# Attention value products with V stationary, two query tiles side by side, sums divided out later

## The chip, the cores and the metric

The kernel runs on one core of a Trainium2 chip. The metric is the device time of one execution in microseconds (us); three runs of the kernel before gave a median of 2039.84 us (2039.72 to 2040.91). The core has a matrix engine (TensorE, PE in the rows; PEld is its weight load), a vector engine (DVE), a scalar engine (ACT), a general engine (POOL), and a sync engine (SP) that here only issues DMAs. Each runs its own list of instructions in order and waits on semaphores that others raise. SBUF is the working memory of 128 partitions, PSUM the memory of 128 partitions into which PE writes.

## The reference, cut to what matters

The program is two transformer-like blocks on one sequence of 1024 tokens with 1024 channels, all in float32. The change is in the attention of the first block and in one product of the second. The attention has 8 heads of 64 channels; three dilated causal windows are combined by the softmax of their log-sums:

```python
sc = jnp.einsum('xhnqd,xhnkd->xhnqk', qb, kb).astype(jnp.float32) * scale
sc = jnp.where(valid, sc + bias[:, None], NEG_INF)
m = jnp.max(sc, axis=-1, keepdims=True)
p = jnp.exp(sc - m)
den = jnp.sum(p, axis=-1, keepdims=True)
o = jnp.einsum('xhnqk,xhnkd->xhnqd', p, vb.astype(jnp.float32)) / den
...
wts = jax.nn.softmax(jnp.stack(lses, axis=0), axis=0)
o_att = jnp.sum(wts[..., None] * jnp.stack(outs, axis=0), axis=0)
y_att = o_att @ w_proj_att
...
merged = jax.nn.sigmoid(g_att + gb_att) * y_att + jax.nn.sigmoid(g_ssm + gb_ssm) * y_ssm
```

Three windows with one softmax over them are one softmax over all causal keys with a bias that counts in how many windows a key lies, and this is how the kernel computes it. In the second block, a causal 128x128 matrix per group mixes the tokens of each chunk:

```python
sg = jnp.einsum('gts,bnsgc->bntgc', w_m, vc) + b_s.T[:, :, None]
```

## The kernel before, in words

Large products run with each float32 operand split into a high and a low part (type fp32r) and take three matmuls per pair of tiles; PE does them in a fixed written order, and POOL and ACT make the split weights ahead of it. The attention stands at 226 to 544 us of the span.

It walks over 64 tiles, `tiles`: a head and a block of 128 queries, `qb` from 0 to 7. A tile needs the `qb + 1` key blocks of 128 up to its own. Before, the tiles of a head go long, short, long, short (7, 0, 6, 1, 5, 2, 4, 3). Tile t goes through these steps, software-pipelined over the engines:

- `scores(t)` on PE (line 1380) writes q times k into PSUM slot t % 2.
- `smallest(t)` on DVE (line 2598) adds the bias and takes the minimum of the negated scores.
- `softmax(t)` on ACT (line 1938) takes the exponential and its sum `den`.
- `transposes(t)` on PE (lines 1394 and 1400) turns each 128x128 block of the weights into slot 2.
- `near_half(t)` on DVE (line 2608, first four blocks of a long tile) and `transposed(t)` on ACT (line 1952, the rest) copy them to SBUF.
- `values(t)` on PE (line 1419) multiplies by V: the turned weights are the stationary 128x128 operand, 64 columns of V move, and 128 queries by 64 channels come out.
- `normalised(t)` on DVE (lines 2614 and 2621) takes the reciprocal of `den` and multiplies into `o_tok`.

In PE's list one iteration t is `scores(t+3)`, `gate_part(t+1)`, `transposes(t+1)`, `values(t)`. A gate part (line 1194) is 12 large matmuls of another product, the gates, interleaved here; two parts fill one PSUM bank, `gate_logits` on ACT (line 1964) reads it, and the next part waits for that (`gate_read`). Every fourth iteration has four small matmuls `ada` (line 1292), whose operand DVE adds up in `ada_chunks` (line 2636). At the end `out_transposes` (line 1437) turns `o_tok` to channels by tokens, and `o_high` on ACT and `o_low` on DVE split it for the projection (`product`, line 1108).

SP's queue (the loop at line 670) issues loads at fixed places of the same loop over t, each behind a wait. Behind the loop it loads `ys_h` and `ys_l` (lines 699 and 700), the output of the state-space branch, whose four landings PE awaits (`y_in`) before the projection; then the gates come back (line 709).

The spatial product of the second block (`spatial`, line 1576) is 16 matmuls in each of four units, V-like operand stationary with 64 columns, group 0 for all eight token tiles and then group 1.

Of the kernel before, what the change touches and what calls it, by code (L numbers as in the profile page):

```python
# [169 lines left out]
def build(nc, a, out):  # L170
    ctx = ExitStack()
    with ctx:
# [110 lines left out]
        prob_long = at("prob_long", [P, 2, T], 160 * kib)  # L283
        prob_short = at("prob_short", [P, 2, HALF], 168 * kib)
        pt_long = at("pt_long", [P, T], 172 * kib)
        pt_short = at("pt_short", [P, HALF], 176 * kib)
        gate_st = at("gate_st", [P, 2, HALF], 178 * kib)
        ada_part = at("ada_part", [P, 2, NB], 182 * kib)
        o_tok = at("o_tok", [P, QB, ATT], 184 * kib)
        neg_max = at("neg_max", [P, 4], 204 * kib)  # L290
        den = at("den", [P, 4], 204 * kib + 32)
        rden = at("rden", [P, 4], 204 * kib + 64)
# [8 lines left out]
        gate_in = at("gate_in", [P, 2, 2, T], 184 * kib)  # L301
# [27 lines left out]
        tiles = [(h, qb) for h in range(HEADS) for long in range(QB - 1, QB // 2 - 1, -1) for qb in (long, QB - 1 - long)]  # L329
# [4 lines left out]
        def prob_of(t):  # L334
            return (prob_short if t % 2 else prob_long)[:, t // 2 % 2, :]

        def prob_t_of(t):
            return pt_short if t % 2 else pt_long
# [12 lines left out]
        v_d = nc.dram_tensor("v_scratch", [QB, P, ATT], F32).ap()  # L351
        ysh_d = nc.dram_tensor("ysh_scratch", [2, P, T], F32).ap()
# [8 lines left out]
            p_ready pt0 pt1 ptc0 ptc1 pv o_ready otr oh_ready ot_ready proj_read mix_ready mh_ready  # L361
# [35 lines left out]

        op_ready = (op_in, later(64)), beyond(f_in[0], 64 + 32 + 32), (op_in, later(64 + 32))
# [98 lines left out]
        def _(sp):  # L497
# [172 lines left out]
            for t in range(NT):  # L670
# [7 lines left out]
                if t in (NT // 4 + 1, NT // 2 + 1):  # L678
                    pair = t // (2 * NH) + 1
                    sp.wait_ge(s["pv"], AHEAD + 2 * NH * (pair - 1))  # L680
# [21 lines left out]
            def gates(j):  # L702
                for th in range(2):
                    sp.wait_ge(gate_out[th], AHEAD + 16 * (KD + 2 * j + 2))
                for cg in range(2):
                    if j:
                        sp.wait_ge(s["proj_read"], AHEAD + 2 * j + cg - 1)
                    for g in range(2):
                        sp.dma_start(gate_in[:, cg, g, :], gates_d[g * KD + 2 * j + cg]).then_inc(gate_back[cg], 16)

            sp.wait_ge(s["otr"], KA)
# [385 lines left out]
        def _(pe):  # L1097
# [84 lines left out]
            def gate_part(i):  # L1182
# [9 lines left out]
                for c in range(KD // 2 * part, KD // 2 * part + KD // 2):  # L1192
                    for p, (w, x) in enumerate(((w_h, act_h), (w_h, act_l), (w_l, act_h))):
                        last = nc.tensor.matmul(slot(1)[:, HALF:T], w[:, n % 2, c, P * (j % 2):P * (j % 2) + P], x[:, c, tok],  # L1194
# [189 lines left out]
            def transposes(t):  # L1384
# [4 lines left out]
                if t % 2:  # L1389
                    pe.wait_ge(s["ptc0"], t // 2 + 1)  # L1390
                elif t:
                    pe.wait_ge(s["ptshort"], t // 2)
# [3 lines left out]
                if qb >= 4:  # L1396
                    if t:
                        pe.wait_ge(s["ptc1"], t // 2)
# [4 lines left out]
            def values(t):  # L1403

                h, qb = tiles[t]
                pair = h // 2
                if qb >= 4:
                    pe.wait_ge(s["ptc0"], t // 2 + 1)
                    pe.wait_ge(s["ptc1"], t // 2 + 1)
                else:  # L1410
                    pe.wait_ge(s["ptshort"], t // 2 + 1)
                if t % (2 * NH) == 0:
                    pe.wait_ge(v_in[pair % 2], 16 * (pair // 2 + 1))
                if t >= 2:
                    pe.wait_ge(s["o_ready"], AHEAD + t - 1)
                dst = slot(3)[:, HALF * (t % 2):HALF * (t % 2) + HALF]
                src = prob_t_of(t)
# [5 lines left out]
                if t % 4 == 3:  # L1423
                    k = t // 4
                    pe.wait_ge(s["ada_summed"], SUMMED + k + 1)
                    ada(dst[:, HD:HD + 2], ada_part[:, k % 2]).then_inc(s["ada_done"], 1)

            for t in range(2):
                scores(t)
            gate_part(0)  # L1430
# [3 lines left out]
            def out_transposes(c, dst):  # L1434

                for t in range(QB):
                    last = nc.tensor.transpose(dst[:, P * t:P * t + P], o_tok[:, t, P * c:P * c + P], ident[:])
                last.then_inc(s["otr"], 1)
# [1779 lines left out]
```

## Time and profile before

| | us |
|---|---|
| median of three runs | 2039.84 |
| profiled execution, its own time | 2037.9 |
| its span, first to last instruction | 2036.2 |
| PE busy in the span | 2004.8 |
| attention, 226 to 544 of the span | 318 |

Busy times of one engine merge instructions that overlap. Matmuls are pipelined, so the mean duration of one is longer than the distance from one start to the next; what a group costs is read from the start of its first to the start of what follows. A float32 matmul leaves two records, each a weight load and a matmul, so 288 products leave 576.

### The profile page before, as it was taken

What the parts mean: (1) busy time and instruction counts of PE and PEld (TensorE: products, weight loads), DVE (VectorE), ACT (ScalarE), POOL (GpSimd) and SP (SyncE); (2) the same over time, 40 slices, a digit from 0 to 9 for tenths busy, and PEclk for the clock granted to TensorE, in tenths of its full rate; (3) what the DMA queues carried; (4) which work ended last, traced back from release to release, by engine and by line L of the source; (5) the groups of instructions that cost most, each with busy time, mean ns of one, the idle gap of its engine ahead of it and who ended that gap; (6) DMA issues with size and microseconds to landing.
All of it is one profiled execution on the core that took longest, in us unless ns stands there. A gap on an engine that the chain in (4) does not pass through costs nothing. (4 is left out here: it accounts for less than half of the span.)

```text
span 2036.2 us, 25850 instructions
## 1 busy us (share of the span) xinstructions
PE 2004.8 (98%) x10079; PEld 1678.1 (82%) x10079; DVE 1070.7 (53%) x1381; ACT 646.8 (32%) x1068; POOL 1303.7 (64%) x757
## 2 busy tenths in 40 slices
PE   7999999999999999999999999999999999999998
PEld 4788988888888887788888888888888888887888
DVE  5971355556472495655622377721563555525554
ACT  4212332232331364444300045433434533311103
POOL 2648445756165539999945456876887888849650
PEclk9999999999999999999999999999999999999999
DMA  9545645444445213233474241343234222098332
GB/s 370 147 104 155 207 136 165 148 142 136 176 145 186 92 43 119 100 112 120 178 289 170 94 145 30 116 141 108 72 115 145 103 104 104 32 355 309 131 135 83
DMA packets 188360, 293.24 MB, mean 144 GB/s; under 512 B 12920, under 2 KB 136784, under 8 KB 188240
## 3 DMA queue, kind: packets, MB, share of 16 engines
q1 hardware_dynamic: 178256, 268.53, 38.9%
q10 hardware_dynamic: 9984, 23.07, 2.9%
q8 instruction: 80, 1.31, 0.3%
q14 instruction: 40, 0.33, 0.1%
HBM read 211.64 MB, written 79.94 MB: 143 GB/s over the span
## 5 line engine op out<-in xcount | busy, mean ns | idle before, releaser
L964 POOL TENSOR_SCALAR w_h<-raw 128x512 fp32r<-128x512 f32 (+2 forms) x108 | 237.0, 2194 | 332.3 <-issue 155.3
L1505 PE MATMUL ps<-tb,w_h 128*128 128x512 f32 x1344 | 416.9, 391 | 4.2 <-DVE quads L2772 3.6
L1050 POOL TENSOR_TENSOR w_l<-raw,w_h 128x512 fp32r<-128x512 f32 x210 | 310.1, 1486 | 99.3 <-ACT w_h L2062 99.3
L1505 PEld LDWEIGHTS ps<-tb,w_h 128*128 128x128 f32 x1344 | 251.3, 188 | 60.8 <-DVE quads L2772 5.2
L1505 PE MATMUL ps<-tb,w_l 128*128 128x512 f32 x672 | 261.6, 389 | 0.0
L966 POOL TENSOR_TENSOR w_l<-raw,w_h 128x512 fp32r<-128x512 f32 (+2 forms) x108 | 200.6, 1857 | 9.0
L2062 ACT ACTIVATE w_h<-raw 128x512 fp32r<-128x512 f32 x210 | 130.8, 628 | 236.1 <-PE ps L1505 153.5
L1505 PE MATMUL ps<-act_h,w_h 128*128 128x512 f32 x504 | 196.3, 389 | 0.6 <-ACT quads L2091 0.5
L1505 PE MATMUL ps<-act_l,w_h 128*128 128x512 f32 x504 | 196.1, 389 | 0.0
L1505 PE MATMUL ps<-act_h,w_l 128*128 128x512 f32 x504 | 196.1, 389 | 0.0
L1505 PEld LDWEIGHTS ps<-tb,w_l 128*128 128x128 f32 x672 | 126.1, 188 | 26.2
L1108 PE MATMUL ps<-act_h,w_h 128*128 128x512 f32 x352 | 139.1, 395 | 2.4 <-POOL w_l L966 1.6
L1108 PE MATMUL ps<-act_h,w_l 128*128 128x512 f32 x352 | 137.1, 389 | 0.0
L1108 PE MATMUL ps<-act_l,w_h 128*128 128x512 f32 x352 | 137.0, 389 | 0.0
L1505 PEld LDWEIGHTS ps<-act_h,w_h 128*128 128x128 f32 x504 | 94.6, 188 | 21.1 <-ACT quads L2091 0.9
L1505 PEld LDWEIGHTS ps<-act_l,w_h 128*128 128x128 f32 x504 | 94.6, 188 | 19.7
L1505 PEld LDWEIGHTS ps<-act_h,w_l 128*128 128x128 f32 x504 | 94.6, 188 | 19.5
L1194 PE MATMUL ps<-act_h,w_h 128*128 128x512 f32 x256 | 100.3, 392 | 0.0
L1194 PE MATMUL ps<-act_l,w_h 128*128 128x512 f32 x256 | 100.1, 391 | 0.0
L1194 PE MATMUL ps<-act_h,w_l 128*128 128x512 f32 x256 | 100.1, 391 | 0.0
L995 POOL TENSOR_SCALAR k_hh<-q 128x1024 fp32r<-128x1024 f32 x8 | 22.2, 2773 | 115.7 <-DMA k_ll<-qk_scratch 115.7
L1050 POOL TENSOR_TENSOR w_l<-sum,w_h 128x512 fp32r<-128x512 f32 x56 | 79.3, 1417 | 20.6 <-ACT w_h L2062 18.8
(412 smaller groups left out, 4554.3 us busy)
## 6 DMA issues: line engine op xcount, KB each, us to landing
raw<-in_w_in SPq DMA_DIRECT2D x44, 1024.0 KB, 5.2
raw<-in_w_up SPq DMA_DIRECT2D x16, 1024.0 KB, 5.2
f_scratch<-r SPq DMA_DIRECT2D x16, 1024.0 KB, 8.2
gates_scratch<-quads SPq DMA_DIRECT2D x24, 512.0 KB, 7.6
r<-gates_scratch SPq DMA_DIRECT2D x12, 1024.0 KB, 7.0
ada_lo<-in_w_ada SPq DMA_DIRECT2D x16, 512.0 KB, 3.6
ada_hi<-in_w_ada SPq DMA_DIRECT2D x16, 512.0 KB, 3.9
gates_scratch<-gate_st ACTq DMA_DIRECT2D x32, 256.0 KB, 2.2
```

The costliest lines, as they stand in the source:

```text
L964: nc.gpsimd.tensor_scalar(w_h[:, k, c, :], src[:, c, :], 1.0, None, ALU.mult).then_inc(s["w_high"], 1)
L966: nc.gpsimd.tensor_tensor(w_l[:, k, c, :], src[:, c, :], w_h[:, k, c, :].bitcast(F32), ALU.subtract).then_inc(done, 1)
L995: stage_step(nc.gpsimd.tensor_scalar(k_hh[:, e, :], q.bitcast(F32), 1.0, None, ALU.mult))
L1050: nc.gpsimd.tensor_tensor(w7_l[:, SLOTS[o]], x, w7_h[:, SLOTS[o]].bitcast(F32), ALU.subtract)\
L1108: last = nc.tensor.matmul(dst[:, tok], w[:, k, kw + c, P * cg:P * cg + P], x[:, c, tok], start=(c == 0 and p == 0), stop=(c == kc - 1 and ...
L1194: last = nc.tensor.matmul(slot(1)[:, HALF:T], w[:, n % 2, c, P * (j % 2):P * (j % 2) + P], x[:, c, tok], start=(c == 0 and p == 0), stop=( ...
L1505: last = nc.tensor.matmul(bank_of(n, bank), w[:, SLOTS[o], c, :], x(c), start=(first and c == 0 and p == 0), stop=(c == KD // 2 - 1 and p ...
L2062: A.activation(w7_h[:, SLOTS[o]], src, ACT.Copy).then_inc(s["w7_high"], 1)
```

## The change

Seven edits:

- The tiles of a head go from long to short, 7 down to 0, and the weights use three buffers by turns.
- `values(u)` takes two neighbouring tiles, 2u and 2u+1. The 64 columns of V are stationary and 128 query columns move; tile 2u's result goes to PSUM partitions 0 to 63, tile 2u+1's to 64 to 127, block by block in turn. The result is channels by queries, so `out_transposes` is gone.
- DVE copies the result undivided to `o_raw` (`read_values`), and the division comes later: every fourth tile DVE takes reciprocals of 4 x 128 sums, SP stores them to memory (`rden_scratch`) and reads them back spread over 64 partitions (`over_den`), and DVE multiplies half a head at a time.
- The gate bank moves from slot 1 to slot 3, and ACT reads it ahead of its copy of the turned weights.
- In the last iterations the gate parts, `o_high`, `o_low` stand elsewhere, and the projection does both `ys` products before the first attention product.
- The gates read back go to two other places in SBUF, with other waits before them.
- `spatial` alternates the two groups within a token tile.

```diff
-        tiles = [(h, qb) for h in range(HEADS) for long in range(QB - 1, QB // 2 - 1, -1) for qb in (long, QB - 1 - long)]
+        tiles = [(h, qb) for h in range(HEADS) for qb in range(QB - 1, -1, -1)]
...
+                if t % 4 == 2:
+                    sp.wait_ge(*beyond(rden_ready, t // 4 + 1))
+                    sp.dma_start(rden_d[t // 4].rearrange("(b p) -> p b", p=P), rden[:, t // 4 % 2, :], allow_slow_non_contiguous=True)                      .then_inc(rden_out[0], 16)
+                if t % 4 == 3:
+                    i = t // 4
+                    sp.wait_ge(*beyond(rden_out, 16 * (i + 1)))
+                    if i:
+                        sp.wait_ge(*beyond(o_norm, i))
+                    sp.dma_start(over_den[head_rows(i // 2), :], rden_d[i].partition_broadcast(HD)).then_inc(rden_in[0], 16)
...
-            sp.wait_ge(s["otr"], KA)
+            sp.wait_ge(s["sm_ready"], AHEAD + NT)
+            sp.wait_ge(s["ot_ready"], 2)
             gates(0)
...
-                for b in range(qb + 1):
-                    last = nc.tensor.matmul(dst[:, 0:HD], src[:, P * b:P * b + P],
-                                            v_st[:, pair % 2, b, HD * (h % 2):HD * (h % 2) + HD],
-                                            start=(b == 0), stop=(b == qb))
+                if u:
+                    pe.wait_ge(s["o_ready"], AHEAD + 2 * u)
+                if u % 2:
+                    pe.wait_ge(s["ada_summed"], SUMMED + u // 2 + 1)
+                    ada(slot(3)[:, P:P + 2], ada_parts[u // 2 % 2]).then_inc(s["ada_done"], 1)
+                elif u:
+                    pe.wait_ge(s["mod2_ready"], u // 2)
+                for b in range(tiles[2 * u][1] + 1):
+                    for i in range(2):
+                        if b <= tiles[2 * u + i][1]:
+                            last = nc.tensor.matmul(slot(3)[HD * i:HD * i + HD, 0:P],
+                                                    v_st[:, pair % 2, b, head_rows(h)], prob_t_of(2 * u + i)[:, P * b:P * b + P],
+                                                    start=(b == 0), stop=(b == tiles[2 * u + i][1]))
...
             for t in range(NT):
                 if t + 3 < NT:
                     scores(t + 3)
                 if t + 1 < NT - 2:
                     gate_part(t + 1)
+                if t >= NT - 2:
+                    gate_part(t)
+                if t % 2:
+                    values(t // 2)
                 if t + 1 < NT:
                     transposes(t + 1)
-                if t == NT - 3:
-                    pe.wait_ge(s["sm_ready"], AHEAD + NT - 1)
-                    pe.wait_ge(s["o_ready"], AHEAD + 2 * NH)
-                    out_transposes(0, slot(0))
-                if t == NT - 2:
-                    gate_part(NT - 2)
-                values(t)
-            pe.wait_ge(s["ptshort"], NT // 2)
-            out_transposes(1, slot(2))
-            gate_part(NT - 1)
-            pe.wait_ge(s["o_ready"], AHEAD + NT)
-            out_transposes(2, slot(3))
-            pe.wait_ge(s["ot_ready"], 2)
-            out_transposes(3, slot(2))
...
-                    product(slot(2 * cg + 1), (N_PROJ + j) % 2, cg, 2, ys_h, ys_l, kw=KA).then_inc(s["gemm"], 1)
-                    first = s["ot_ready"] if j == 0 and cg == 0 else None
-                    product(slot(2 * cg), (N_PROJ + j) % 2, cg, KA, o_h, o_l, each=first).then_inc(s["gemm"], 1)
+                        pe.wait_ge(s["mod2_ready"], NT // 4)
+                    product(slot(2 * cg + 1), (N_PROJ + j) % 2, cg, 2, ys_h, ys_l, kw=KA)
+                    if j:
+                        product(slot(2 * cg), (N_PROJ + j) % 2, cg, KA, o_h, o_l).then_inc(s["gemm"], 2)
+                if j == 0:
+                    for cg in range(2):
+                        product(slot(2 * cg), N_PROJ % 2, cg, KA, o_h, o_l, each=None if cg else s["ot_ready"]).then_inc(s["gemm"], 2)
...
-                for g in range(2):
-                    grp = 2 * c + g
-                    for t in range(QB):
+                for t in range(QB):
+                    for g in range(2):
+                        grp = 2 * c + g
...
+                if t % 2 == 0 and t < NT - 2:
+                    gate_logits(t // 2)
                 if t + 1 < NT:
                     transposed(t + 1)
-                if t % 2 == 0 and t < NT - 2:
-                    gate_logits(t // 2)
                 if t + 2 < NT:
                     softmax(t + 2)
...
-                if t % 2 and t + 1 < NT:
-                    near_half(t + 1)
                 if t + 3 < NT:
                     smallest(t + 3)
                 ada_chunks(t // 4, ((0, 1, 2), (3, 4, 5), (6, 7), ())[t % 4])
-                normalised(t)
-                if t == NT - 3:
-                    o_low(0, slot(0))
-            o_low(1, slot(2))
-            o_low(2, slot(3))
-            o_low(3, slot(2))
+                if t % 4 == 2:
+                    over_denominators(t // 4)
+                if t % 2:
+                    read_values(t // 2)
+                if t + 1 < NT and is_long(t + 1):
+                    near_half(t + 1)
+                if t % 4 == 1 and t >= 4:
+                    normalised(t // 4 - 1)
+                if t >= NT - 2:
+                    o_low(t - (NT - 2))
+            normalised(NT // 4 - 1)
+            for c in range(2, KA):
+                o_low(c)
```

How instructions stand on three engines, before and now. First PE in the middle of a head, without the 12 gate matmuls between the groups. Before, transposes of a short tile (`prob_short`), the value products of a long one (five blocks), and scores of a later one:

```order
L1394 MATMUL ps<-ident,prob_short 128x128 x4
L1419 MATMUL ps<-v_st,pt_long 128x64 x5
L1380 MATMUL ps<-k_hh,q_124 128x512
L1380 MATMUL ps<-k_ll,q_124 128x512
L1380 MATMUL ps<-k_hh,q_124 128x384
```

Now, in an odd iteration, the last gate matmul of a part, the value products of two tiles (four and three blocks), the transposes of the next tile, and scores:

```order
L1220 MATMUL ps<-act_h,w_l 128x512
L1449 MATMUL ps<-prob_t,v_st 64x128 x7
L1418 MATMUL ps<-ident,prob 128x128 x2
L1406 MATMUL ps<-k_hh,q_124 128x512
L1406 MATMUL ps<-k_ll,q_124 128x512
```

The value products moved ahead of the transposes, stand only in every second iteration, and have output shape 64x128 in place of 128x64. Next ACT in the same region, where `gate_st` is the read of the gate bank, `pt_long` and `pt_short` (now `prob_t`) the copies of the turned weights. Before:

```order
L1952 ACTIVATE pt_short<-ps 128x256 [waits pv,pt0]
L1964 ACTIVATE gate_st<-ps,cols_a 128x512 [waits gemm,gate_out1]
L1938 ACTIVATE prob_long,den<-prob_long,neg_max 128x768 [waits o_ready,sm_ready]
L1952 ACTIVATE pt_long<-ps 128x256 [waits pv,pt1]
L1938 ACTIVATE prob_short,den<-prob_short,neg_max 128x384 [waits o_ready,sm_ready]
L1971 DMA gates_scratch<-gate_st 128x512 [waits gate_read]
```

Now:

```order
L1980 ACTIVATE gate_st<-ps,cols_a 128x512 [waits gemm,gate_out1]
L1968 ACTIVATE prob_t<-ps 128x128 [waits pv,pt1]
L1954 ACTIVATE prob,den<-prob,neg_max 128x512 [waits sm_ready]
L1968 ACTIVATE prob_t<-ps 128x512 [waits pv,pt0]
L1954 ACTIVATE prob,den<-prob,neg_max 128x384 [waits sm_ready]
L1987 DMA gates_scratch<-gate_st 128x512 [waits gate_read]
```

The gate read moved from behind the copy to ahead of it. Last, SP's queue at the end of the attention, where `ada_hi` is a load of the small products, `ys_h` and `ys_l` the state-space output. Before:

```order
L632 DMA ada_hi<-in_w_ada 128x4x256 [waits ada_summed]
L640 DMA raw<-in_w_proj_att 128x4x256 [waits w_split]
L642 DMA raw<-in_w_proj_ssm 128x2x256
L699 DMA ys_h<-ysh_scratch 128x1024 [waits y_spill,s_ready]
L700 DMA ys_l<-ysl_scratch 128x1024
```

Now (`colt_read` is the semaphore of `rden_ready`, `const_in` that of `rden_out`, `c_ready` that of `o_norm`):

```order
L656 DMA raw<-in_w_proj_att 128x4x256 [waits w_split]
L658 DMA raw<-in_w_proj_ssm 128x2x256
L714 DMA over_den<-rden_scratch 64x512 [waits c_ready,const_in]
L708 DMA rden_scratch<-rden 128x4x1 [waits colt_read]
L714 DMA over_den<-rden_scratch 64x512 [waits c_ready,const_in]
L724 DMA ys_h<-ysh_scratch 128x1024 [waits y_spill,s_ready]
L725 DMA ys_l<-ysl_scratch 128x1024
```

The last two stores and spreads of the sums now stand between the last weight load and the `ys` loads.

## Rows read from the trace of the kernel before

**Rows 1.** Page, engines: busy time, share of the span, instructions

```profile
PE 2004.8 (98%) x10079; PEld 1678.1 (82%) x10079; DVE 1070.7 (53%) x1381; ACT 646.8 (32%) x1068; POOL 1303.7 (64%) x757
```

**Rows 2.** Windows: us, busy us of each engine (instructions), clock, DMA share, GB/s

```profile
300.00:340.00 40.00, 40.00 (x243) 35.08 (x242) 24.99 (x56) 12.37 (x30) 23.54 (x9) 1.00 0.52 162
1340.00:1362.30 22.30, 22.30 (x116) 18.58 (x114) 4.59 (x6) 7.55 (x13) 14.46 (x12) 1.00 0.38 118
```

**Rows 3.** Groups by line: records, busy us, mean ns of one, idle before

```profile
L1419 PE MATMUL ps<-v_st,pt_long 128*128 128x64 f32 x416 | 50.0, 271 | 0.0
...
L1419 PE MATMUL ps<-v_st,pt_short 128*128 128x64 f32 x160 | 21.4, 265 | 0.0
...
L1236 PE MATMUL ps<-u_c,drive 128*64 128x128 f32 x64 | 3.7, 274 | 0.0
```

**Rows 4.** Timeline, PE: value products; columns start us, us, engine, line, operation, tiles

```profile
387.55 1.00 PE L1419 MATMUL ps<-v_st,pt_short 128*128 128x64 f32 x8
388.39 0.56 PE L1292 MATMUL ps<-ones,ada_part 128*128 128x1 f32 x4
...
391.99 1.90 PE L1419 MATMUL ps<-v_st,pt_long 128*128 128x64 f32 x16
393.70 0.48 PE L1380 MATMUL ps<-k_hh,q 128*128 128x512 f32 x1
```

**Rows 5.** Timeline, PE: state-space input, 64 columns stationary, column halves alternating

```profile
105.80 0.39 PE L1108 MATMUL ps<-act_h,w_l 128*128 128x512 f32 x1
106.12 3.71 PE L1236 MATMUL ps<-u_c,drive 128*64 128x128 f32 x64
109.77 0.50 PE L1108 MATMUL ps<-act_h,w_h 128*128 128x512 f32 x1
110.10 0.40 PE L1108 MATMUL ps<-act_l,w_h 128*128 128x512 f32 x1
```

**Rows 6.** Timeline, PE: one unit of the spatial products

```profile
1339.81 3.33 PE L1576 MATMUL ps<-wst,vg 128*64 128x128 f32 x32
1343.07 0.73 PE L1505 MATMUL ps<-tb,w_h 128*128 128x512 f32 x2
```

**Rows 7.** Timeline, PE: the last gate matmul, the transposes behind it, the projection

```profile
542.64 0.39 PE L1194 MATMUL ps<-act_h,w_l 128*128 128x512 f32 x1
542.87 1.91 PE L1437 MATMUL ps<-ident,o_tok 128*128 128x128 f32 x16
544.54 0.47 PE L1108 MATMUL ps<-ys_h,w_h 128*128 128x512 f32 x1
```

**Rows 8.** Timeline, ACT and PE: PE waiting for ACT, and ACT for PE

```profile
531.27 0.20 ACT L1938 ACTIVATION_READ_ACCUMULATOR prob_long<-prob_long,neg_max 128x1 f32 x1
...
531.52 0.66 PE L1394 MATMUL ps<-ident,prob_long 128*128 128x128 f32 x4 [0.68 <-ACT prob_long L1938]
...
543.13 0.69 ACT L1964 ACTIVATE gate_st<-ps,cols_a 128x512 f32<-128x512 f32 x1 [1.81 <-PE ps L1194]
```

**Rows 9.** Timeline, DVE at the end of attention

```profile
535.90 1.00 DVE L2636 SCALAR_TENSOR_TENSOR ada_part<-ada_hi,c_act,ada_part 128x256 f32<-128x256 f32 x2
...
538.28 0.28 DVE L2621 TENSOR_SCALAR o_tok<-ps,rden 128x64 f32<-128x64 f32 x1
...
541.36 1.23 DVE L2655 TENSOR_TENSOR o_l<-ps,o_h 128x1024 fp32r<-128x1024 f32 x1 [1.57 <-ACT o_h L1976]
```

**Rows 10.** Timeline, SP's queue: first and last of the four ys loads

```profile
526.50 0.34 SPq L699 DMA_DIRECT2D ys_h<-ysh_scratch  x1
...
527.83 0.43 SPq L700 DMA_DIRECT2D ys_l<-ysl_scratch  x1
```

**Rows 11.** The ys_l loads (line 700), time to landing

```profile
DMA to landing us min/median/max: 4.5/5.6/6.6
```

**Rows 12.** DMA issues: KB each, median us from issue to landing

```profile
taps_scratch<-taps_s SPq DMA_DIRECT2D x8, 16.0 KB, 1.8
```

**Rows 13.** PE's longest wait: us in total, times, longest us

```profile
PE ps L1274 <- DMA x_tok<-in_x: 3.8, 1, 3.8
```

More of the change, by code:

```diff
@@ L334, in prob_of, with is_long, longs, shorts @@
         def prob_of(t):
-            return (prob_short if t % 2 else prob_long)[:, t // 2 % 2, :]
+            return prob[:, (t + 2) % 3, :]
         def prob_t_of(t):
-            return pt_short if t % 2 else pt_long
+            return prob_t[:, t % 2, :]
+        def is_long(t):
+            return tiles[t][1] >= 4
+        def longs(t):
+            return sum(is_long(i) for i in range(t + 1))
+        def shorts(t):
+            return t + 1 - longs(t)
+        def head_rows(h):
+            return slice(HD * (h % 2), HD * (h % 2) + HD)
+        def token_half(i):
+            return slice(0, HALF) if i % 2 else slice(HALF, T)
         ps = ctx.enter_context(nc.psum_tensor("ps", [P, 4, T], F32))
@@ L679, in _ @@
                     pair = t // (2 * NH) + 1
-                    sp.wait_ge(s["pv"], AHEAD + 2 * NH * (pair - 1))
+                    sp.wait_ge(s["pv"], AHEAD + NH * (pair - 1))
                     for k in range(2):
@@ L1401, in transposes, with values @@
                     last.then_inc(s["pt1"], 1)
-            def values(t):
-                h, qb = tiles[t]
+            def values(u):
+                t = 2 * u + 1
+                h = tiles[t][0]
                 pair = h // 2
-                if qb >= 4:
-                    pe.wait_ge(s["ptc0"], t // 2 + 1)
-                    pe.wait_ge(s["ptc1"], t // 2 + 1)
-                else:
-                    pe.wait_ge(s["ptshort"], t // 2 + 1)
-                if t % (2 * NH) == 0:
+                if is_long(t):
+                    pe.wait_ge(s["ptc0"], longs(t))
+                    pe.wait_ge(s["ptc1"], longs(t))
+                else:
+                    pe.wait_ge(s["ptshort"], shorts(t))
+                if t // (2 * NH) != (t - 2) // (2 * NH):
@@ L2606, in near_half @@
                 if t >= 2:
[L2607 to L2622 removed]
+                    dve.wait_ge(s["pv"], AHEAD + t // 2)
@@ new lines, in near_half, with read_values @@
+                v.tensor_copy(prob_t_of(t)[:, 0:HALF], slot(2)[:, 0:HALF]).then_inc(s["ptc0"], 1)
+            def read_values(u):
+                h = tiles[2 * u][0]
+                dve.wait_ge(s["pv"], AHEAD + u + 1)
+                for i in range(2):
+                    qb = tiles[2 * u + i][1]
+                    v.tensor_copy(o_raw[head_rows(h), h // 2, P * qb:P * qb + P],
+                                  slot(3)[HD * i:HD * i + HD, 0:P]).then_inc(s["o_ready"], 1)
+                if u % 2:
+                    lo = 2 * N_ADA_EARLY + 2 * (u // 2)
+                    dve.wait_ge(s["ada_done"], ADA_DONE + u // 2 + 1)
+                    v.tensor_tensor(mod[:, lo:lo + 2], slot(3)[:, P:P + 2], col_a("b_ada", lo, 2), ALU.add)\
+                     .then_inc(s["mod2_ready"], 1)
@@ new lines, in over_denominators, with normalised @@
+            def over_denominators(i):
+                h, lo = i // 2, 0 if i % 2 else QB // 2
+                dve.wait_ge(s["p_ready"], 4 * i + 4)
+                if i >= 2:
+                    dve.wait_ge(*beyond(rden_out, 16 * (i - 1)))
+                v.reciprocal(rden[:, i % 2, :], den[:, h % 2, lo:lo + QB // 2]).then_inc(rden_ready[0], 1)
+            def normalised(i):
+                h = i // 2
+                x = o_raw[head_rows(h), h // 2, token_half(i)]
+                dve.wait_ge(*beyond(rden_in, 16 * (i + 1)))
+                dve.wait_ge(s["o_ready"], AHEAD + 4 * i + 4)
+                v.tensor_tensor(x, x, over_den[head_rows(h), :], ALU.mult).then_inc(o_norm[0], 1)
@@ L2624, in ada_chunks @@
             def ada_chunks(k, chunks):
-                part = ada_part[:, k % 2]
+                part = ada_parts[k % 2][:]
                 for c in chunks:
```

114 lines of the change are left out of this document (44 added, 70 removed).

## The prediction, made before the changed kernel was run

> **What bounds the kernel now.** I read the page's busy times first [rows 1]: PE is busy 98% of the span, POOL 64%, DVE 53%. The windows then say whether this holds where the change is: in 40 us in the middle of the attention PE has no idle time while DVE has 25.0 us and ACT 12.4 us of work, and in a spatial unit PE is again full with POOL at 14.5 of 22.3 us [rows 2]. So a microsecond taken out of PE's list there is a microsecond of the kernel, until something else makes PE wait. What is to be seen next in the timeline is the price of PE's pieces (start to start) and, at the end of the attention, which loads PE finds ready.
>
> **Value products, removed form.** Eight records take from 387.55 to 388.39, sixteen from 391.99 to 393.70 [rows 4]: 24 in 2.55 us, 0.106 us each. There are 416 + 160 = 576 [rows 3], so 61.2 us.
>
> **Value products, new form.** The trace has no value product of this shape, but it has the form twice. Line 1236 has 64 stationary columns, 128 moving ones and output halves that alternate from product to product: 64 records, of which the last starts 3.71 - 0.27 = 3.44 us after the first [rows 3, 5], 0.0546 us apart. Line 1576 has the same shape with one half eight times in succession: 3.33 - 0.27 over 31 distances, 0.0987 us [rows 6]. I take 0.0546 where both tiles have a block and 0.0987 for the last block of the longer tile, which has no partner. Per head there are four groups with 7, 5, 3 and 1 pairs and one block over: 16 pairs x 4 records x 0.0546 = 3.49 us, 4 x 2 x 0.0987 = 0.79 us.
>
> Each group also pays for going into and out of the half-width form. In rows 5 the first one starts 0.32 us behind the last 512-wide matmul instead of 0.23 [rows 7], the next form starts 0.21 us behind the last one instead of 0.055, and its second matmul 0.33 instead of 0.23 later: 0.09 + 0.155 + 0.10 = 0.345 us. Four groups: 1.38 us. A head takes 5.66 us, eight heads 45.3 us: 15.9 us less. Bounds: no price for the change of form and everything as in the pairs would leave 31.4 us; all at 0.0987 with the price 67.9 us. I stay at the rows of line 1236, which agree in shape, type and alternation; only the accumulation over blocks is new.
>
> The Trainium skill, "TensorEngine Tiling (Array Packing)", Key Properties, says that a change of tiling mode drains the engine; the gaps of rows 5 agree with it, and without them the saving would read 26.9 us.
>
> **Spatial products.** 32 records take 3.26 us [rows 6]; alternating, 32 x 0.0546 + 0.155 = 1.90 us. Four units: 5.4 us less. PE is full there [rows 2], so it stays.
>
> **Gone and new at the end of the loop.** The 32 `out_transposes` go: 16 take 1.67 us [rows 7], so 3.3 us. The wait of 0.68 us at 531.52 [rows 8] goes with the old order of the tail. New: in iteration 61 no gate part stands between `transposes(61)` and `values(30)`, and ACT reads the gate bank before it copies that tile. With S the start of the last gate matmul, ACT begins 0.49 us later (542.64 to 543.13) and takes 0.69 us [rows 7, 8]; with a copy of 384 columns, by the 0.69 us of 512 about 0.5, PE goes on at S + 1.7 instead of S + 0.5: 1.2 us more.
>
> **Gate read.** In the loop the same read ends at S + 1.18, and PE starts 0.05 us after ACT (531.47 to 531.52) [rows 8]: S + 1.23. PE's own work until the next gate part is the transposes of tile t+1 and the scores of tile t+4. In the new order the four even iterations of a head have 7, 5, 3 and 1 transposes (0.104 us each) and 4, 2, 8 and 6 key blocks of scores (two matmuls per 512 columns at 0.23 us [rows 7], so 0.3 to 0.9 us). For t = 2 and 6 of each head that ends near S + 1.1. PE waits about 0.13 us, and loads the first weights uncovered, 0.1 us as in rows 5. 15 such places: 3.4 us more. Bounds: nothing, and 15 x 0.69 = 10 us if the read stood free. Before, a long value product lay in between. Queued behind the wait is PE's whole list.
>
> **Division later.** On DVE the copies (two of 0.28 us at most [rows 9]) replace reciprocal and multiplication; a multiplication of half a head is half of 1.23 us [rows 9]. This lies beside PE: DVE has 15 of 40 us free [rows 2]. DVE waits in place for `over_den`, with the next minimum behind it, but the scores of that tile are needed only two iterations later, some 9 us, so a microsecond or two there costs nothing.
>
> **The ys loads.** These decide the end. Before, SP issued the four at 526.50 to 527.83 and the last landed up to 6.6 us after its issue, 534.4 [rows 10, 11]; PE came at 544.54 [rows 7]. Now they stand behind the last store and spread of the sums. Count from V, the end of `values(30)`. DVE: two copies 0.56, half-head product 0.62, two `ada` steps 1.00 [rows 9], reciprocal at most 0.28: V + 2.5. Store of 8 KB to landing as the 16 KB one of 1.8 us [rows 12]: V + 4.3. One issue step of 0.44 us (1.33 / 3 in rows 10) for the spread: V + 4.7. Four loads as before, 7.9 us from first issue to last landing: V + 12.7. PE meanwhile: three transposes 0.3, two gate parts of 12 matmuls at 0.23 us 5.4, `ada` 0.4, `values(31)` 0.4, changes of form 0.7: V + 7.2. PE waits 5.5 us, where it waited for nothing. Bounds 3 us (loads landing in 5.5) and 9 us (a store of 512 pieces of 4 bytes, which no row shows, taking twice as long as the 16 KB row and the spread in front of the loads delaying them). The spread sums themselves are needed only behind both `ys` products, another 5.4 us, so their chain is covered by the same wait.
>
> PE idle that long may lose granted clock. The rows show 1.00 after idling up to 3.8 us [rows 2, 13] and nothing longer. Between nothing and all 24 `ys` matmuls at half speed (5.4 us) I take 1.4 us, near the row that shows no fall.
>
> **Sum.** -15.9 - 5.4 - 3.3 - 0.7 + 1.2 + 3.4 + 5.5 + 1.4 = -13.8 us. The profiled execution took 2037.9 us, 1.9 under the median of the runs; against it 2024.1, and with the same difference the median becomes 2026.0 us.
>
> **Rivals.**
>
> A. The two halves do not overlap, for instance because a weight load for one half waits for the matmul in the other. Every record then costs 0.0987 us: 56.9 + 11.0 = 67.9 us for the value products, 6.7 more than before; nothing is won in the spatial products; with the other terms (-3.3 - 0.7 + 1.2 + 3.4 + 5.5 + 1.4 = +7.5) it is +14.2, 2054 us, slower. It decides from 0.079 us per record on, where 576 records and the 128 spatial ones together win nothing. Against it: 0.0546 in rows 5; for it only that line 1236 does not accumulate. 5%.
>
> The Trainium skill, "TensorE: Matmul & The Clock Gate", Part 3, says that weight loads overlap running matmuls only when the row group differs; here both halves use all rows and differ in columns, so by that rule rival A holds and the time is 2054 us. Rows 5 speak against the rule: column halves alternate there at 0.0546 us.
>
> B. The `ys` loads are in time, because DVE or the DMAs run further ahead than I count: 6.9 us less, 2019 us. For it: all four loads wait for nothing but their turn in SP's queue. Against it: that turn. 15%.
>
> C. The sums come back late within the heads: every second spread stands behind a weight load that waits for POOL, and if its landing takes as long as a `ys` load (4.5 to 6.6 us [rows 11]) DVE stands still. Once that exceeds the two iterations of slack PE waits. At 1.2 us in each of eight heads, 2036 us; at 2.5 us, 2046. 8%.
>
> D. The tail and the gate waits both reach their upper bounds and eat the gain (+3.5 and +6.6): 2036 us. Against it: the read has 0.9 us of other work in front of PE in every place. 4%.
>
> **How the numbers follow.** Forecast 68%, with its own range of 2019 to 2034 (the pair rate 10% either way 3.5 us, gate waits 0 to 6, `ys` wait 3 to 9). With B whole and the near half of C and D, 80% and a little over lie between 2016 and 2037. A difference under 0.2%, 4.1 us, cannot be told from none by three runs of this kernel. Faster (under 2035.8): forecast, B and a part of C and D, 0.87. Same: 0.07. Slower: A and the far part of C, 0.06.
>
> **What would show it.** Value products: groups of 30, 22, 14 and 6 records lasting about 2.1, 1.6, 1.2 and 0.8 us with their changes of form; at twice that, A. Spatial: 32 records in 1.9 us. Gate read: waits of PE for ACT's gate line in two of four even iterations, 0.1 to 0.2 us. End: one PE wait of 3 to 9 us before the first `ys` product, ended by a `ys_l` load; none means B. DVE's waits for `over_den` without a PE wait behind them; with one, C. The forecast fails if PE idles more than 15 us between 226 and 550.

## The result and the profile after

The changed kernel took 2045.17 us (median of 9 runs, 2042.41 to 2051.65), the kernel before 2040.56 us beside it (9 runs, 2039.72 to 2041.72): ratio 1.003, 95% interval 1.0022 to 1.0038. The forecast was 2026.0 with a range of 2016 to 2037; the change made the kernel slower, by 4.6 us between the medians. The profiled execution took 2044.87 us.

The first row of the page answers to [rows 1]: PE has 32 records and 19.3 us less to do, and yet the span grew, so its share fell from 98 to 97%.

```profile
PE 1985.5 (97%) x10047; PEld 1642.6 (80%) x10047; DVE 1082.4 (53%) x1349; ACT 648.1 (32%) x1068; POOL 1305.6 (64%) x757
```

The products themselves came out as forecast. PE's timeline of the changed kernel (start us, us, engine, line, operation, tiles; line 1449 is the value product, line 1591 the spatial one):

```profile
305.01 0.65 PE L1449 MATMUL ps<-prob_t,v_st 128*64 128x128 f32 x6
305.59 0.66 PE L1418 MATMUL ps<-ident,prob 128*128 128x128 f32 x4
...
313.71 0.39 PE L1220 MATMUL ps<-act_h,w_l 128*128 128x512 f32 x1
314.02 1.96 PE L1449 MATMUL ps<-prob_t,v_st 128*64 128x128 f32 x30
315.92 0.66 PE L1418 MATMUL ps<-ident,prob 128*128 128x128 f32 x4
...
1353.14 1.97 PE L1591 MATMUL ps<-wst,vg 128*64 128x128 f32 x32
1355.04 0.73 PE L1520 MATMUL ps<-tb,w_h 128*128 128x512 f32 x2
```

Thirty value records take 1.90 us, where 24 took 2.55 [rows 4]; 32 spatial ones take 1.90 instead of 3.26 [rows 6]. So PE got its microseconds. They went into PE's waits. The list of waits in the attention (engine, tile, line, what ended the wait: us in total, times, longest) is short before, 1.4 us in all, the second of the two being the wait in [rows 8]:

```profile
PE ps L1380 <- ACT qkv_st L1879: 0.7, 1, 0.7
PE ps L1394 <- ACT prob_long L1938: 0.7, 1, 0.7
```

After:

```profile
PE ps L1134 <- DMA ys_l<-ysl_scratch: 17.2, 1, 17.2
PE ps L1318 <- DVE prob_t L2621: 5.0, 4, 1.9
PE ps L1418 <- DVE prob_t L2621: 3.1, 2, 2.8
PE ps L1318 <- DVE ada_part L2665: 3.0, 3, 1.8
PE ps L1449 <- ACT prob_t L1968: 0.9, 1, 0.9
```

That is 17.2 us at the end and 11.1 us in the loop for DVE. The prediction's own sign of failing, more than 15 us of idle time of PE between 226 and 550, has come. A window of the loop shows the second: 2.1 us without PE work where there were none [rows 2].

```profile
300.00:340.00 40.00, 37.93 (x240) 31.20 (x239) 22.59 (x50) 11.96 (x28) 23.70 (x9) 1.00 0.59 162
```

DVE's waits, same columns, say what DVE was late for: the spread sums, and the `ada` loads that SP issued late:

```profile
DVE o_raw L2651 <- DMA over_den<-rden_scratch: 47.1, 15, 10.2
...
DVE ada_part L2665 <- DMA ada_hi<-in_w_ada: 17.9, 5, 7.4
```

SP's waits lead to the common cause, the store of the reciprocals (`rden_scratch`), for which SP stands still before it may issue the spread:

```profile
SPq L714 <- DMA rden_scratch<-rden: 114.5, 13, 14.8
```

SP's queue at the end (one issue per row) shows it where no other transfer of this queue is in the way, and answers to [rows 10]:

```profile
539.30 0.37 SPq L708 DMA_DIRECT2D rden_scratch<-rden  x1
547.98 0.45 SPq L714 DMA_DIRECT2D over_den<-rden_scratch  x1
548.53 0.53 SPq L724 DMA_DIRECT2D ys_h<-ysh_scratch  x1
549.11 0.42 SPq L725 DMA_DIRECT2D ys_l<-ysl_scratch  x1
549.59 0.42 SPq L724 DMA_DIRECT2D ys_h<-ysh_scratch  x1
550.05 0.94 SPq L725 DMA_DIRECT2D ys_l<-ysl_scratch  x1
```

From the store's issue to the next issue 8.7 us pass. The windows of that time (columns as in [rows 2]; the last two are DMA share and GB/s) show that the DMAs do nothing in most of it: the pieces move within the microsecond from 540 on, then a gate store ends, then there is silence until the store is reported done.

```profile
540.00:541.00 1.00, 0.67 (x7) 0.41 (x7) 0.67 (x2) 0.53 (x1) 0.96 (x1) 1.00 0.25 2
541.00:543.00 2.00, 0.00 (x0) 0.00 (x0) 1.59 (x3) 0.00 (x0) 1.92 (x2) 1.00 0.34 131
543.00:547.90 4.90, 0.00 (x0) 0.00 (x0) 0.00 (x0) 0.00 (x0) 4.82 (x3) 0.57 0.00 0
```

PE comes back at 557.89, and answers to the last row of [rows 7] as follows; the first seven products stand 0.43 us apart instead of 0.23 (at half the granted clock, 1.2 of 2.4 GHz; 0.53 in the window from 557.5 to 561), 1.4 us in all:

```profile
540.02 0.65 PE L1449 MATMUL ps<-prob_t,v_st 128*64 128x128 f32 x6
557.89 0.79 PE L1134 MATMUL ps<-ys_h,w_h 128*128 128x512 f32 x1 [17.22 <-DMA ys_l<-ysl_scratch]
558.48 0.63 PE L1134 MATMUL ps<-ys_l,w_h 128*128 128x512 f32 x1
558.91 0.63 PE L1134 MATMUL ps<-ys_h,w_l 128*128 128x512 f32 x1
```

### The profile page after: what moved, and what is told of

The parts are those of the page before. It is cut to its first block and busy times, and to the rows that moved or that the text cites. A ratio compares the mean times of both kernels' runs of the same rounds, so it can differ in the third digit from the quotient of the medians.

```text
span 2043.1 us, 25773 instructions
## 1 busy us (share of the span) xinstructions
PE 1985.5 (97%) x10047; PEld 1642.6 (80%) x10047; DVE 1082.4 (53%) x1349; ACT 648.1 (32%) x1068; POOL 1305.6 (64%) x757
## 5 line engine op out<-in xcount | busy, mean ns | idle before, releaser
L2924 DVE SCALAR_TENSOR_TENSOR h_t<-ps,mod,h_t 128x1024 f32<-128x1024 f32 x28 | 36.0, 1284 | 107.7 <-PE ps L1626 102.0
```

The lines of the kernel that those rows point to most:

```text
L2924: v.scalar_tensor_tensor(h_t[:, u, :], slot(u % 4), mod[:, 5 * KD + u:5 * KD + u + 1], h_t[:, u, :], ALU.mult, ALU.add).then_inc(s["down_r ...
```

## The experiments

Three explanations were set against each other. Theory T: the store of the sums, 512 pieces of 4 bytes, takes 8 us and more; SP, DVE's `over_den` and the ys loads are late behind it. R1: the idle time in the loop comes from the new order of tiles. R2: the pieces hold up all other loads, whether anybody waits for the store or not. The kernel before, run beside each set, had medians between 2038.3 and 2041.8 us; ratios are to it.

**The ys loads ahead of the last store.**

```diff
+                if t == NT - 2:
+                    (the two waits and the four ys loads)
                 if t % 4 == 2:
                     sp.wait_ge(*beyond(rden_ready, t // 4 + 1))
                     sp.dma_start(rden_d[t // 4]...
```

> The changed kernel with the four ys loads issued in iteration 62, in front of the last store of the sums, instead of behind its spread. Theory T (the store of the sums, 512 pieces of 4 bytes, takes 8 to 15 us, and what stands behind it in SP's queue or behind DVE's wait comes late): PE's wait of 17.2 us for ys_l goes; the next one is for the last heads' normalised values, which DVE finished at about 555.9 in the changed kernel; PE reaches them at about 548, so 7 us of wait remain, and most of the half clock goes: 2034 us, 11 less than the changed kernel; the idle time of about 13 us within the loop stays. Rival R1 (the loop's idle time comes from the new order of the tiles, not from the sums) says the same of this run. Rival R2 (the 4-byte pieces hold up all other loads): the ys loads, now in flight together with the last store, land late as well, wait 10 us or more, 2040 us.

Measured: 2032.86 us, ratio 0.9967 (0.9946 to 0.9989), 12.3 less than the changed kernel. PE waited 1.6 us for `ys_l` and then 3.8 for the low halves of the last values. R2's 2040 is out for this place: the two `ys_l` loads, issued ahead of the store, land 5.9 and 8.7 us after their issue (before 4.5 and 6.6 [rows 11]). The waits for DVE in the loop mostly stayed, 8.3 of 11.1 us.

**The sums turned on TensorE, stored in 4 pieces of 512 bytes.**

```diff
+                nc.tensor.transpose(slot(3)[0:QB // 2, 2 * P:3 * P], den[:, h % 2, lo:lo + QB // 2], ident[:])
...
-                v.reciprocal(rden[:, i % 2, :], den[:, h % 2, lo:lo + QB // 2])
+                v.reciprocal(rden[:], slot(3)[0:QB // 2, 2 * P:3 * P])
...
-                sp.dma_start(rden_d[t // 4].rearrange("(b p) -> p b", p=P), rden[:, t // 4 % 2, :], ...
+                sp.dma_start(rden_d[t // 4].rearrange("(b p) -> b p", p=P), rden[:])
```

The edit also makes PE wait for the reciprocal, and DVE takes it behind its two copies instead of ahead of them.

> The changed kernel with the sums turned on TensorE first (16 more transposes, 128 x 4 to 4 x 128), so that each store of the reciprocals has 4 pieces of 512 bytes instead of 512 pieces of 4. Everything else as in the changed kernel. T: SP's 13 waits for the store fall from 114.5 us to under 40, DVE's 15 waits for over_den from 47 us to under 15, PE's idle time in the loop from about 13 us to under 5, the wait for ys_l from 17.2 to about 7 us; 16 transposes cost 1.7 us: 2027 us. R1: the waits of SP and DVE fall, but PE's idle time in the loop stays at about 13 us: 2036 us. R2: as T.

Measured: 2030.25 us, ratio 0.9938 (0.9916 to 0.9959), 14.9 less. SP's waits for the store fell to 33.1 us, DVE's for `over_den` to 17.8, PE's for `ys_l` to 8.6. In the loop PE waited 4.7 us, for a wait that this edit adds (PE for the reciprocal), and no longer for DVE's copies: R1 fails. The new place of the reciprocal on DVE could have helped the copies too; the shortest repair below leaves DVE's order alone, and there PE does not wait for the copies either.

**No store, and a store that nobody waits for.** Both spread an old row; the first has neither the store nor DVE's wait for it.

```diff
-                    sp.wait_ge(*beyond(rden_out, 16 * (i + 1)))
-                    sp.dma_start(over_den[head_rows(i // 2), :], rden_d[i].partition_broadcast(HD))
+                    sp.dma_start(over_den[head_rows(i // 2), :], ysl_d[0, 8 * i, 0:HALF].partition_broadcast(HD))
```

> The changed kernel without the store of the reciprocals; the spread reads a row that has long been in memory instead (so the products are not divided by the sums of their exponentials). T: the idle time in the loop falls from about 13 us to under 4 us, the ys loads leave SP by about 541 and PE waits at most 3 us for them: 2019 us. R1: the loop's 13 us stay, the ys wait goes: 2030 us. R2: as T.

> As the one before (the spread reads an old row, no division by the sums), but the stores of the reciprocals in 4-byte pieces are issued as in the changed kernel; only SP's wait for them goes. T: waiting is the cost, not the traffic, so within 3 us of the kernel without the store: 2020 us. R2: the 4096-byte loads next to the stores land as late as in the changed kernel (k_ll 8.8, q 8.2, bias 9.8 us), the loop's idle time stays above 8 us, and the time is 2030 us or more. R1: 2030 us.

Measured: 2024.17 us (ratio 0.9908, 0.9887 to 0.9928) without the store and 2038.28 us (0.9994, 0.9981 to 1.0007; ten runs from 2033.5 to 2044.7) with it, 14.1 apart. T had these equal and is wrong in this: of the 21.0 us between the changed kernel and the one without the store, only 6.9 go with the waits; 14.1 are there when nothing waits for it. R2 is right on the larger part, but not on where it named it: PE waited 5.1 us for DVE in the loop, where R2 had over 8. PE's listed waits explain most of the difference: 17.8 us for DVE and `ys_l` with the store, 7.0 without it, 10.8 apart in the two profiled executions (2033.5 us, the fastest of ten, and 2026.0, the slowest of four). Windows of the unawaited store at the end (the store is issued at 528.57, the ys loads from 529.60 to 531.11):

```profile
529.00:530.00 1.00, 1.00 (x7) 0.83 (x6) 0.65 (x1) 0.76 (x2) 0.00 (x0) 1.00 0.25 2
530.00:531.00 1.00, 1.00 (x6) 0.84 (x5) 0.00 (x0) 1.00 (x2) 0.00 (x0) 1.00 0.65 145
531.00:539.00 8.00, 1.85 (x15) 1.44 (x13) 2.10 (x5) 1.10 (x2) 6.61 (x4) 0.81 1.03 39
539.00:545.50 6.50, 0.00 (x0) 0.00 (x0) 4.54 (x4) 2.34 (x2) 1.46 (x1) 0.50 0.98 378
```

The same loads without the store, from their issue to their landing:

```profile
529.68:538.00 8.32, 4.98 (x29) 4.01 (x28) 4.99 (x8) 2.96 (x5) 4.01 (x2) 1.00 0.89 306
```

From 531 to 539, behind the store, the DMA engines count as fully busy and move 39 GB/s; then 378. This is called the hold below. The `ys_l` loads land after

```profile
DMA to landing us min/median/max: 12.2/13.3/14.4
```

and PE waits 12.7 us for them, against 3.3 without the store:

```profile
PE ps L1133 <- DMA ys_l<-ysl_scratch: 12.7, 1, 12.7
PE ps L1130 <- DMA ys_l<-ysl_scratch: 3.3, 1, 3.3
```

**Both repairs**, the first two edits together.

> The sums turned on TensorE and stored in 4 pieces of 512 bytes, and the ys loads issued in iteration 62, ahead of the last store. Theory T' (the store of 512 pieces of 4 bytes holds SP, DVE's over_den and every load queued behind it for 8 to 10 us; with it gone, and the ys loads ahead, nothing of the new order is slower): of the 2030.3 us of the kernel with the turned sums alone, the 8.6 us for ys_l fall to at most 2: 2023 us, range 2019 to 2027. Rival R3 (the sums' way through memory is late at the end whatever the size of the pieces): PE then waits 4 us or more for the low halves of the values instead, 2028 us or more.

Measured: 2019.68 us, ratio 0.9893 (0.9875 to 0.9911). The gains of the two repairs add up (12.3 + 14.9 = 27.2; 25.5 together). PE waits neither for `ys_l` nor for the low halves: R3 fails.

**What the pieces must be.** From the kernel whose store nobody waits for: 128 pieces of 16 bytes (the edit below), and 512 pieces of 4 issued by ACT.

```diff
-                    sp.dma_start(rden_d[t // 4].rearrange("(b p) -> p b", p=P), rden[:, t // 4 % 2, :], ...
+                    sp.dma_start(rden_d[t // 4].rearrange("(p b) -> p b", p=P), rden[:, t // 4 % 2, :], ...
```

> As the kernel whose stores of the reciprocals nobody waits for (the spread reads an old row, no division by the sums; 2038.3 us, against 2024.2 without the stores), but each store has 128 pieces of 16 bytes instead of 512 of 4. Theory P (the hold grows with the number of pieces): a quarter of the 14 us is left, 2028 us, and the last ys load lands about 10 us after the first is issued. Theory F (any store of small pieces holds the queue for the same 8 to 10 us): 2038 us, ys loads landing after 12 to 13 us as with 4-byte pieces.

> The same kernel (spread of an old row, no division by the sums) with the stores of 512 pieces of 4 bytes issued by ACT in iterations 3, 7, 11 and so on, in the queue that also carries the gate logits, instead of by SP. Theory Q (the hold is the order within one queue): the loads on SP's queue are not held, 2025 us, ys_l landing in 5 to 7 us; the gate stores land later instead. Theory M (the DMA engines or the memory are held, whatever the queue): 2036 to 2040 us, ys_l landing after 10 us or more where a store runs beside it.

Measured: 2023.17 us (ratio 0.9917, 0.9899 to 0.9934) with 128 pieces, within the noise of the kernel without the store: neither P's quarter nor F's fixed hold. PE's wait for `ys_l` is 6.1 us against 3.3 without it. On ACT's queue 2062.9 us (1.0116, 1.0099 to 1.0132), 25 slower than on SP's, beyond what M expected; Q fails. PE's waits there:

```profile
PE ps L1314 <- DVE ada_part L2664: 19.9, 6, 3.8
PE ps L1130 <- DMA ys_l<-ysl_scratch: 12.2, 1, 12.2
```

The `ys_l` loads show the hold across the queues. SP issued them at 558.31 and 559.26, ACT its last store at 559.08; PE starts at 574.81, with the landing of the second:

```profile
DMA to landing us min/median/max: 7.4/11.4/15.5
```

So the hold is not the order within one queue. Against the kernel whose stores stand in SP's queue, PE's waits are 14.3 us longer, and PE's list between them takes 13.9 us more, at a mean granted clock of 0.91 from 340 to 460 us where the other has 1.00. Why the waits grow when ACT issues the stores, no run here shows.

The Trainium skill, "DMA: Bandwidth & Descriptors", Specifications, puts the limit below which a transfer is read, changed and written back at 512 bytes. Both 4 and 16 bytes lie under it, and the page names no difference between them; here they differ by 15 us, and the runs decide.

**The spatial order alone, on the kernel before.**

```diff
-                for g in range(2):
-                    grp = 2 * c + g
-                    for t in range(QB):
+                for t in range(QB):
+                    for g in range(2):
+                        grp = 2 * c + g
```

> The kernel before with the changed order of the spatial products alone (its two halves alternate). The prediction's term: 32 records in 1.90 us instead of 3.26, four units, 5.4 us less than before: ratio 0.9973. Rival: PE waits for POOL or for the next list instead, or the records don't get closer without the rest of the change: within 1 us of before.

Measured: 2034.40 us, ratio 0.9970 (0.9960 to 0.9979): 6.1 us of 2041.6 (4.3 to 8.2 by the interval), with 5.4 forecast. The rival fails.

**The halves in turn**, from the kernel with both repairs.

```diff
-                for b in range(tiles[2 * u][1] + 1):
-                    for i in range(2):
+                for i in range(2):
+                    for b in range(tiles[2 * u][1] + 1):
```

> The kernel with turned sums and early ys loads, but the value products of the two query tiles one after the other (all blocks of the first tile, then all of the second) instead of alternating. If the alternation of the two column halves is what makes 512 of 576 records 0.0546 us apart (the prediction's term), they go back to 0.0987 us: 512 x 0.044 = 22.5 us more than the kernel it is made from, less up to 4 us that waits of PE gave anyway: 2043 us. Rival: the gain comes from the 64 stationary columns alone, whatever the order: no change, 2023 us.

Measured: 2032.75 us, ratio 0.9961 (0.9948 to 0.9974), 13.1 more than with alternation. Its 30 records take 3.04 us (to the row behind them) instead of 1.90:

```profile
319.34 3.11 PE L1451 MATMUL ps<-prob_t,v_st 128*64 128x128 f32 x30
322.38 0.66 PE L1419 MATMUL ps<-ident,prob 128*128 128x128 f32 x4
```

From start to next start, summed over all 576 records, the value products take 39.6 us alternating and 56.7 in turn. The alternation is what pays. The expected 22.5 us was too much: with the ends of the groups counted in, a record costs 0.069 us alternating and 0.098 in turn. Of the 17.1 us, 2.3 came back, because PE waited less for the reciprocals, first alternating, then in turn:

```profile
PE ps L1319 <- DVE rden L2652: 2.8, 3, 1.4
PE ps L1319 <- DVE rden L2652: 0.5, 1, 0.5
```

**The gate read behind the copy**, from the same kernel.

```diff
-                if t % 2 == 0 and t < NT - 2:
-                    gate_logits(t // 2)
                 if t + 1 < NT:
                     transposed(t + 1)
+                if t % 2 == 0 and t < NT - 2:
+                    gate_logits(t // 2)
```

> The kernel with turned sums and early ys loads, with ACT's read of the gate logits behind the copy of the next tile's transposes, as in the kernel before, instead of ahead of it. The prediction's reading: the gate read sets when PE's next gate part starts; with a copy of 0.3 to 0.7 us in front of it, PE waits about 0.5 us more in 30 places: 15 us more than the kernel it is made from, 2038 us. Rival: PE has enough other work in between (transposes, scores): at most 2 us more.

Measured: 2032.33 us, ratio 0.9959 (0.9944 to 0.9974), 12.7 more where 15 was expected and the rival had 2, and PE's waits name it:

```profile
PE ps L1221 <- ACT gate_st L1990: 13.5, 30, 0.7
```

**The shortest repair of the changed kernel**, complete:

```diff
+                if t == NT - 2:
+                    (the two waits and the four ys loads)
-                    sp.dma_start(rden_d[t // 4].rearrange("(b p) -> p b", p=P), ...
+                    sp.dma_start(rden_d[t // 4].rearrange("(p b) -> p b", p=P), ...
-                v.tensor_tensor(x, x, over_den[head_rows(h), :], ALU.mult)
+                x = x.rearrange("p (b q) -> p b q", q=P)
+                v.tensor_tensor(x, x, over_den[head_rows(h), :].rearrange("p (q b) -> p b q", q=P), ALU.mult)
```

> The changed kernel with two edits, nothing left out: the reciprocals are stored in the order of the lanes, 128 pieces of 16 bytes, and DVE reads the spread row with a stride of 4 elements; and the ys loads are issued in iteration 62, ahead of the last store. Theory T' (after the runs so far: 512 pieces hold the DMAs, 128 don't): as the kernel with the sums turned on TensorE and early ys loads, ratio 0.989 to before, 2017 to 2022 us, no wait of PE over 3 us in the attention. Rival: DVE's product with a stride of 16 bytes or a store of 16-byte pieces that SP waits for (not only issues) holds DVE in the loop, 2025 us or more.

Measured: 2018.64 us (2014.23 to 2022.76, 5 runs), ratio 0.9886 (0.9871 to 0.9902), level with the kernel of both repairs. SP still waits 50.3 us in ten places for the stores, at most 7.9, but PE hardly pays for it. One of its PE waits is over the expected 3 us:

```profile
PE ps L1319 <- DVE ada_part L2667: 4.7, 2, 3.5
PE ps L1450 <- ACT prob_t L1969: 0.9, 1, 0.9
```

PE now goes from the last value product straight into the ys products:

```profile
532.78 0.65 PE L1450 MATMUL ps<-prob_t,v_st 128*64 128x128 f32 x6
533.39 0.47 PE L1135 MATMUL ps<-ys_h,w_h 128*128 128x512 f32 x1
```

**The stores alone, in the kernel before.**

```diff
+                if t % 4 == 2:
+                    sp.wait_ge(s["p_ready"], t + 2)
+                    sp.dma_start(rden_d[t // 4].rearrange("(b p) -> p b", p=P), ident[:, 0:4], ...
```

> The kernel before with 16 stores of 512 pieces of 4 bytes of a constant, at the places of SP's list where the changed kernel has them, which nothing waits for. Theory T' (a store holds the loads behind it for 8 to 10 us, and this costs what PE needs of them within that time): in the loop 4 to 5 us as in the changed kernel with unawaited stores; the ys loads, here behind the last store too, had 10 us to spare and use them up: 2043 us, 2 to 6 above before. Rival (the stores cost as much in any kernel, by themselves): 14 us or more above before.

Measured: 2049.26 us, ratio 1.0036 (1.0022 to 1.0051): 7.5 more than before, between the two. `ys_l` lands after 13.0/14.1/15.2 us (before 4.5/5.6/6.6 [rows 11]), and that is PE's only new wait; the loop has none:

```profile
PE ps L1112 <- DMA ys_l<-ysl_scratch: 5.7, 1, 5.7
```

Not all of it is the hold. The store of iteration 62 first waits for ACT, so the `ys` loads leave SP only at 537.22 to 538.67, 10.7 us later than before, while PE reaches their place 3.7 us later, at 548.2. With landings as before the last would have come at 545.3, ahead of PE; the 8.6 us that it lands later make the wait. A store costs what PE needs soon of the loads behind it.

## Why the prediction was wrong

**The step that failed** is the store: "Store of 8 KB to landing as the 16 KB one of 1.8 us" [rows 12]. It has 2 KB, so the size given was wrong too, but the number of bytes was not the point: it has 512 pieces of 4 bytes, and 8.7 us passed where nothing else was in SP's queue. The prediction named the pieces, and still took twice the 16 KB row as the longest that they could last. Measured, the wait for the ys loads was 17.2 us, not 5.5 with bounds of 3 and 9. Counted from the end of `values(30)` at 533.69, as the prediction counts, the 11.7 us more are:

- 3.1 us ahead of the store, issued at 5.6 instead of 2.5: DVE stood 2.98 us for the spread before, which was late behind the store before.
- 6.9 us in the store, 8.7 instead of 1.8.
- 1.5 us behind it, in the issue of the spread and the four loads, and PE came 0.2 us earlier than forecast.

```profile
532.68 1.09 PE L1449 MATMUL ps<-prob_t,v_st 128*64 128x128 f32 x14 [0.89 <-ACT prob_t L1968]
533.69 0.44 PE L1418 MATMUL ps<-ident,prob 128*128 128x128 f32 x2
537.46 0.69 DVE L2651 TENSOR_TENSOR o_raw<-o_raw,over_den 64x512 f32<-64x512 f32 x1 [2.98 <-DMA over_den<-rden_scratch]
```

**The second step** came from the first: "DVE waits in place for `over_den`... a microsecond or two there costs nothing". The wait was up to 10.2 us, 47.1 in all, and DVE's copies and `ada` sums came late for PE: 11.1 us. That is rival C's mechanism, which had 8%; it counted a landing of 4.5 to 6.6 us on top of a short store. Part of the 11.1 us is the hold: DVE's waits for `ada_hi` are 17.9 us in the changed kernel, 8.1 where nothing waits for the store, and 1.3 without the store.

**The sum.** The profiled execution was forecast at 2024.1 and took 2044.87, 20.8 more. The ys wait is 11.7 over its term, the loop's waits 11.1 over nothing, 22.8 together; by subtraction the other terms came out about 2 better.

**What held.** Value products: the groups of 30, 22, 14 and 6 take 1.90, 1.45, 1.02 and 0.58 us, forecast 2.1, 1.6, 1.2 and 0.8; the forecast has in it 0.19 us a group that such a distance leaves to the neighbours. From the first score product to the first ys product, PE's waits taken off, the kernel before takes 317.8 us and the shortest repair 300.4: 17.4 less, where value products, `out_transposes` and gate waits were to give 15.8. Spatial: 5.4 forecast, 6.1 measured alone. The tail wait: 0.9, forecast 1.2 (it took the place of 0.7). Rival A falls with the groups: in turn 3.04 us, alternating 1.90. By the rule of the Trainium skill, "TensorE: Matmul & The Clock Gate", Part 3, which the prediction names beside rival A, the two orders would be alike; here they are not, and the runs decide.

The gate read held too, though no wait in PE's list names it. In the shortest repair the first gate matmul stands 0.16 to 0.29 us late behind the scores in 15 places, two of every four even iterations, and the next one mostly 0.07 to 0.11 us later; about 5 us in all, where 3.4 was forecast, and about 3 in the kernel of both repairs. One such place in the changed kernel, where the two distances are 0.33 and 0.34 us instead of 0.11 and 0.23:

```profile
522.74 0.28 PE L1406 MATMUL ps<-k_ll,q 128*128 128x256 f32 x1
523.07 0.50 PE L1220 MATMUL ps<-act_h,w_h 128*128 128x512 f32 x1
523.41 0.40 PE L1220 MATMUL ps<-act_l,w_h 128*128 128x512 f32 x1
```

**What was luck.** The clock: 1.4 us forecast, seven distances 0.2 us too long measured. The 1.4 was a choice between nothing and 5.4 for a wait of 5.5 us, and the wait that it came out for was 17.2.

**What the forecast would have been** with the ys loads in time and no hold: rival B's 2019. The shortest repair took 2018.6; in part that is chance, since the kernel before beside it took 2041.8 and so the gain is 23.2 us, where rival B has 20.8.

## What to carry to other kernels

Before a transfer goes onto a path that others share, count its pieces and their size, not only its bytes, and look for a row with pieces like them; if there is none, the upper bound is open, and everything behind it in the program belongs into that bound. When a change makes the bounding engine faster, put the loads it needs next ahead of any new wait in the queue that issues them. Small results that must go across the partitions can be stored partition by partition, in the order in which they lie, and put right by the access pattern of the reader.

## What the hardware showed that was not expected

A store of 512 pieces of 4 bytes moves its data in about a microsecond, is reported done 8.7 us after its issue, and for 8 us the loads behind it run at 39 GB/s instead of about 306, with the DMA engines counted as busy. The loads are held also where nothing waits for the store (14.1 of the 21.0 us), and another queue does not help: 2062.9 us from ACT's. The same 2 KB in 128 pieces of 16 bytes cost nothing clear of the noise (2023.2 against 2024.2 us), though they too take 3.9 us to land (median of 16). Number and size of the pieces, and the order in which neighbouring partitions write into memory, changed together, and nothing between was tried, so which of them makes the hold, and where it sets in, stays open.
